# One mixer block in another order: inputs first, gates inside the recurrence, a chunked state space branch

## The chip, the cores and the metric

One core of a Trainium2 chip runs the whole program. The time is device microseconds of one execution, compared by the median of several. Engines run their own queues in order and meet at semaphores: TensorE (PE), VectorE (DVE), ScalarE (ACT), GpSimd (POOL) and SyncE (SP), which issues DMAs.

## The reference

Two transformer blocks at 512 tokens and width 1024. The change lies in the first one's mixer:

```
mod = silu(c) @ ada_w + ada_b            # six groups of 1024: sh1, sc1, gt1, sh2, sc2, gt2
h = rms_norm(x) * (1 + sc1) + sh1
p = h @ w_in                             # inputs of four branches, and four gates of 1024
y_a = rwkv7(...)                         # state S (64x64 a head, 4 heads):
                                         #   S = S*w_t + (S a_t) b_t^T + v_t k_t^T ; o_t = S r_t
y_b = spatial_gating(...)                # gelu, layer norm, a 128x128 causal mix per chunk
y_c = short_conv(...)                    # three taps
y_d = s5(...)                            # 1024 complex states: x_t = a x_{t-1} + B u_t ;
                                         #   y = Re(C x) + d u ; then gelu, a gated projection
merged = sum_i sigmoid(gate_i) * y_i
x = x + gt1 * (merged @ w_o)
```

Then a feed-forward layer with modulation by sh2, sc2 and gt2, and a second block of two layers that the change leaves as it is.

## The kernel before

Activations lie transposed, as 8 tiles of 128 features by 512 tokens. A product is made in three matmuls per 128x128 weight block (high times high, high times low, low times high part; `product`, L1280). Weights come as a stream of pieces of 128x1024, 24 matmuls each: POOL loads the high part, negates it and adds the weights in a second DMA, four slots ahead. The order of the pieces is written out by hand (`mixer_pieces`, L54) and each engine's program follows it. Results go through PSUM banks 0 to 3 in turn; `product` waits until the tile four before has been taken out by its owner. Banks 4 to 7 serve the small matmuls.

Every instruction of DVE and ACT is followed by a wait for itself (`do`), so each of them does one thing at a time. `need` waits for the next count of a semaphore.

The modulation weights `ada` come as 48 slabs of 128x1024, eight for each of the six groups, through four slots; SP loads the next when a slot is free. DVE multiplies each with a column of silu(c) and adds them up (`modulate`, L441), and PE adds the partitions with one-column matmuls (`modulation`, L1310). Groups 0 and 1 come before the first norm, group 2 after the recurrence (after `rw_out`), 3 and 4 beside the output projection, 5 in the feed-forward.

The order in the mixer: conv, gating and state space inputs (12 pieces), the gating branch's layer norm and mix, set-up of the state space branch (transposes, masks and tables of cosines and sines by doubling to length 512 on DVE). Then `for s in range(S5T)`: for each of 8 groups of 128 states PE makes the inputs, DVE rotates, scans over 512 tokens and rotates back, and PE reads out; gates and outputs of the conv and gating branches stand between (`BESIDE`, L65). Then the 7 recurrence inputs, their preparation, padded copies, blocks of small matmuls, a triangular solve of 31 steps on DVE with a transposition through DRAM on either side, and the recurrence over 16 chunks of 32 tokens, all of whose small products are made by PE and copied by DVE (heads 0 and 1) and ACT. Gates and outputs of the state space branch and of the recurrence stand before and after these chains. `gated` (L836) multiplies a branch's tile with its gate and adds it to `merged`.

Of the kernel before, what the change touches and what calls it, by code (L numbers as in the profile page):

```python
# [28 lines left out]
C = 32  # L29
# [8 lines left out]
S5T = 8  # L38

# [79 lines left out]
def build(nc, A, out):  # L119
# [6 lines left out]
    with ExitStack() as ctx:  # L126
# [24 lines left out]
        arena = sb("arena", [P, ARENA])  # L151
        eye_r = sb("eye_r", [P, P], F32R)
# [7 lines left out]
        t_dram = nc.dram_tensor("pair_inverse", (2, H_A, NCK, C // 2, C), F32, kind="Internal").ap()  # L160

# [26 lines left out]

        def gate_room(p):

            at = (ARENA - 4 * T, ARENA - 4 * T, ARENA - 5 * T, 2048 if p < 28 else 4096)[p // 8] + p % 4 * T
            return arena[:, at:at + T]

        merged, product, glu = x, work[:, 0, :], work[:, 1, :]
        ada_m = place([("sum", (2, D)), ("ada", (ADA, D))], at=ARENA - (ADA + 2) * D)
        conv_m = place([("bg", (2, T)), ("cg", (2, T)), ("z", (2, T)), ("y", (2, T))])
        sg_m = place([("z", (4, T)), ("mu", (T,)), ("d", (2, T)), ("sq", (2, T)), ("std", (T,)), ("rstd", (T,)),
                      ("vn", (2, T)), ("vt", (2, 4, P)), ("ws", (4, P)), ("wsm", (4, P)), ("bs", (2, P)),
                      ("mix", (2, T)), ("caus", (P,))], at=4096)
        s5_m = place([("ct", (8, T)), ("st", (8, T)), ("w", (6, T)), ("bt", (2, 8, P)), ("bpad", (2, 8, P)),  # L200
                      ("bb", (2, 8, 16)), ("b_in", (2, 8, 16)), ("m8", (8, 8)), ("c_in", (2, 2, P)), ("u", (2, T))])
        s5_m["cc"] = s5_m["bpad"]
        assert s5_m["end"] <= ARENA - 4 * T
# [9 lines left out]
                       at=max(rw_in["end"], rw_bd["end"]))  # L213
# [34 lines left out]
        def _(sp):  # L248
# [3 lines left out]
            for q in range(ADA):  # L252
                sp.dma_start(ada[:, q, :], A["ada"][q]).then_inc(S(f"ada_in{q}"), 16)
# [733 lines left out]
        def _(act):  # L987
# [114 lines left out]
            for k in range(4):  # L1102
                gate()
# [656 lines left out]
```

## Time and profile before

| | us |
|---|---|
| median of 3 runs (lowest, highest) | 2542.22 (2538.32, 2545.75) |
| the profiled execution | 2537.91 |
| its span | 2536.1 |
| PE busy | 2212.2 (87%) |
| DVE busy | 1420.2 (56%) |
| POOL busy | 845.3 (33%) |
| ACT busy | 441.1 (17%) |
| mean granted TensorE clock | 0.922 |

Busy shares are means over stages with different limits. The first block's mixer takes somewhat over a quarter of the span; the rest is feed-forward, attention and a second block. A granted clock of 1.0 is TensorE's 2.4 GHz, 0.5 is 1.2 GHz.

### The profile page before, as it was taken

The page shows a single profiled execution, that of the slowest core. Times are in us where ns is not written, and L with a number is a line of the kernel's source. Part 1 is how long each engine was busy: PE and PEld are TensorE (multiplying, and loading weights), DVE is VectorE, ACT ScalarE, POOL GpSimd, SP SyncE. Part 2 cuts the span into 40 slices and gives each one's busy share as a digit, 9 for nine tenths or more (in the row PEclk, how much of TensorE's full clock was granted, in tenths as well). Part 3 has the DMA queues.
Part 4 walks back from the last instruction along what each step waited for, and adds up shares of the span by engine and source line. Part 5 has one row for each costly group of instructions (what it writes and reads, how often), then busy time and mean ns, then how long its engine had stood idle before and what let it go on. Part 6 is the DMA issues. An engine that isn't in the chain of part 4 may idle for free.

```text
span 2536.1 us, 26355 instructions
## 1 busy us (share of the span) xinstructions
PE 2212.2 (87%) x10172; PEld 1736.6 (68%) x10172; DVE 1420.2 (56%) x1964; ACT 441.1 (17%) x871; POOL 845.3 (33%) x1009
## 2 busy tenths in 40 slices
PE   1967999668787999999988999999898679999995
PEld 1745667557665888887854787878677338878784
DVE  6459775763567344256545572736563665727364
ACT  1010002101000000021056220201210562202021
POOL 1312333110232444444410444444433004444442
PEclk9978999875797999999987999999999789999998
DMA  7635667530695999998820898989877108989895
GB/s 252 135 65 108 141 136 164 96 80 1 174 298 152 205 193 196 191 193 179 183 61 1 193 193 181 195 177 196 194 163 174 31 1 187 193 179 194 182 194 125
DMA packets 115269, 390.31 MB, mean 154 GB/s; under 512 B 20516, under 2 KB 21412, under 8 KB 114632
## 3 DMA queue, kind: packets, MB, share of 16 engines
q0 software_dynamic: 96624, 350.46, 64.8%
q1 hardware_dynamic: 18520, 38.16, 4.3%
q8 instruction: 81, 1.33, 0.2%
q14 instruction: 44, 0.36, 0.0%
HBM read 385.88 MB, written 2.62 MB: 153 GB/s over the span
## 4 chain that ended last, share of the span: by engine, by line
PE 72%; DVE 17%; DMA 5%; ACT 3%; issue 2%; POOL 0%; SPq 0%; DVEq 0%; ACTq 0%
PE ps L1290 61%; DMA arena<-in_ada 3%; PE ps L1379 2%; PE ps L1360 2%; PE ps L1395 1%; DMA w_lo<-in_w 1%; DVE small L706 1%; DVE arena L450 1%; ACT arena L1231 1%; PE ps L1517 1%; ACT arena L1239 1%; DVE work L555 1%; DVE h_lo L367 1%; DVE arena L733 1%; PE ps L1476 1%
## 5 line engine op out<-in xcount | busy, mean ns | idle before, releaser
L1290 PE MATMUL ps<-h_hi,w_hi 128*128 128x512 f32 x1760 | 713.6, 405 | 39.0 <-DVE h_lo L367 27.9
L1290 PE MATMUL ps<-h_lo,w_hi 128*128 128x512 f32 x1760 | 695.7, 395 | 0.0
L1290 PE MATMUL ps<-h_hi,w_lo 128*128 128x512 f32 x1760 | 694.6, 395 | 0.0
L330 POOL DMA_DIRECT2D w_hi<-in_w x334 | 185.7, 556 | 1516.0 <-PE ps L1290 1515.2
L1290 PEld LDWEIGHTS ps<-h_hi,w_hi 128*128 128x128 f32 x1760 | 336.7, 191 | 132.6 <-DVE h_lo L367 28.3
L1290 PE MATMUL ps<-g_hi,w_hi 128*128 128x512 f32 (+1 forms) x880 | 345.6, 393 | 52.0 <-DVE g_lo L367 21.7
L1290 PEld LDWEIGHTS ps<-h_lo,w_hi 128*128 128x128 f32 x1760 | 337.2, 192 | 74.2 <-issue 6.9
L1290 PEld LDWEIGHTS ps<-h_hi,w_lo 128*128 128x128 f32 x1760 | 336.9, 191 | 71.8
L335 POOL TENSOR_SCALAR w_lo<-w_hi 128x1024 fp32r<-128x1024 f32 x334 | 358.6, 1074 | 35.9 <-DMA w_hi<-in_w 30.1
L1290 PE MATMUL ps<-g_lo,w_hi 128*128 128x512 f32 (+1 forms) x880 | 341.6, 388 | 0.0
L1290 PE MATMUL ps<-g_hi,w_lo 128*128 128x512 f32 (+1 forms) x880 | 341.1, 388 | 0.0
L338 POOL DMA_DIRECT2D w_lo<-in_w x334 | 300.4, 899 | 106.0 <-POOL w_lo L335 106.0
L1290 PEld LDWEIGHTS ps<-g_hi,w_hi 128*128 128x128 f32 x880 | 169.4, 192 | 97.0 <-DVE g_lo L367 24.3
L1290 PEld LDWEIGHTS ps<-g_hi,w_lo 128*128 128x128 f32 x880 | 169.6, 193 | 33.3
L1290 PEld LDWEIGHTS ps<-g_lo,w_hi 128*128 128x128 f32 x880 | 169.5, 193 | 32.6 <-issue 0.7
L1256 ACT ACTIVATE arena<-arena,vec 128x512 f32<-128x512 f32 x88 | 71.8, 816 | 412.2 <-DVE arena L728 404.7
L739 DVE TENSOR_TENSOR x<-ps,x 128x512 f32<-128x512 f32 x48 | 33.2, 692 | 183.9 <-PE ps L1290 183.9
L733 DVE SCALAR_TENSOR_TENSOR arena<-arena,vec 128x511 f32<-128x511 f32 x88 | 113.9, 1294 | 3.6 <-ACT arena L1256 0.6
L728 DVE TENSOR_TENSOR arena<-ps,work 128x512 f32<-128x512 f32 x88 | 60.9, 692 | 91.9 <-PE ps L1290 90.5
L960 DVE TENSOR_TENSOR arena<-arena 128x512 f32<-128x512 f32 x32 | 50.3, 1570 | 77.7 <-ACT arena L1178 77.7
L966 DVE SCALAR_TENSOR_TENSOR x<-ps,mod,x 128x512 f32<-128x512 f32 x32 | 24.0, 751 | 111.6 <-PE ps L1290 111.5
L366 DVE CAST g_hi<-arena 128x512 fp32r<-128x512 f32 (+1 forms) x100 | 80.6, 806 | 6.3 <-ACT arena L1112 2.9
(343 smaller groups left out, 2126.7 us busy)
## 6 DMA issues: line engine op xcount, KB each, us to landing
w_hi<-in_w POOLq DMA_DIRECT2D x334, 512.0 KB, 3.9
w_lo<-in_w POOLq DMA_DIRECT2D x334, 512.0 KB, 5.6
arena<-in_ada SPq DMA_DIRECT2D x48, 512.0 KB, 8.8
x<-in_xT SPq DMA_DIRECT2D x1, 2048.0 KB, 17.3
x<-in_xT SPq DMA_DIRECT2D x4, 512.0 KB, 4.7
arena<-in_memT SPq DMA_DIRECT2D x2, 1024.0 KB, 5.4
out_y<-arena SPq DMA_DIRECT2D x1, 2048.0 KB, 6.3
work<-in_mask_dil SPq DMA_DIRECT2D x1, 640.0 KB, 5.9
```

The source lines that it names most:

```text
L330: pool.dma_start(w_hi[:, q % SLOTS, :], A["w"][q]).then_inc(S(f"high_in{q % SLOTS}"), 16)
L335: pool.tensor_scalar(w_lo[:, q % SLOTS, :], w_hi[:, q % SLOTS, :].bitcast(F32), -1.0, 0.0, ALU.mult, ALU.add).then_inc(S("negated"), 1)
L338: pool.dma_start(w_lo[:, q % SLOTS, :], A["w"][q], accum_op=ALU.add).then_inc(S(f"low_in{q % SLOTS}"), 16)
L366: do(dve.tensor_copy(hi, src))
L728: do(dve.tensor_tensor(cv_m["z"][:, side, :], tile()[:], rstd, ALU.mult), "conv_scaled")
L733: do(dve.scalar_tensor_tensor(dst[:, 1:], z[:, :T - 1], w(1), dst[:, 1:], ALU.mult, ALU.add))
L739: update = lambda k: do(dve.tensor_tensor(x[:, k, :], tile()[:], x[:, k, :], ALU.add), "x_done")
L960: do(dve.tensor_tensor(s, r, r, ALU.mult), "relu_used")
L1256: do(act.activation(c[:, j % 2, :], cv_m["z"][:, side, :], ACT.Identity, scale=V("cw2", at), bias=V("cb2", 44 * layer + 22 * side + j0 + j ...
L1290: mm = pe.matmul(bank, w[:, slot, cols], a(k), start=(k == 0 and i == 0), stop=(k == blocks - 1 and i == 2))
L1360: mm = pe.matmul(bank(g)[:, 0:width], at_m["q"][half(g), pair, P * qb:P * qb + P], keys, start=True, stop=not fox)
L1379: mm = pe.matmul(ps[6 + pair % 2][64 * g:64 * g + 64, q0:T], values, pt[pair % 2][:, g, b, q0:T], start=(b == 0), stop=(b == blocks - 1))
```

## The change

- The pieces come in another order: all 19 input pieces first, then gates and outputs.
- Modulation groups 0, 1 and 2 are made by PE alone: `modulation_piece` multiplies each slab as it lies in its slot with a column of silu(c), 8 matmuls of one column, and sums over 8 slabs in PSUM. Groups 0 and 1 are split 12 and 4 slabs, with state space set-up between. Group 2's transfers start after the last chunk, and PE takes its slabs after the last branch output.
- `norm` has its rounding to the high part, with the shift, done by ACT (`high_shifted`); DVE makes the low part. Both norms of the first block use it.
- The state space branch works in chunks of 8 tokens: within a chunk by a Toeplitz matrix (made by matmuls from powers of the step, and spread through DRAM), between chunks by one rotate, scan, rotate back over 64 chunks for all 8 groups of states at once, 512 columns. Its input and its output are turned through DRAM, by one transfer out and 16 in each time. The tables are 64 long.
- In the recurrence PE issues after each of a chunk's three stages a step of six 512-column matmuls of gates and outputs; DVE and ACT have a step of the gating between their copies, with some turns skipped. The chain's first products move from banks 0 and 1 to 4 and 5.
- Single gate pieces stand between the blocks of small matmuls; nine pieces stand before the recurrence instead of four. Clearing the padded tiles moves from DVE (8192 elements, and 2048 later) to ACT.
- Buffers in the arena are laid out anew, with one more tile of 512.

```diff
 def mixer_pieces():
-    order = [("conv_in", 6), ("sg_in", 4), ("s5_in", 2)]
-    for branch in ("conv", "sg"):
-        order += [(branch + "_gate", 4), (branch + "_out", 1)] * 2
-    order += [("rwkv_in", 7)] + [("s5_gate", 4), ("s5_out", 2)] * 2
-    return order + [("rwkv_gate", 4), ("rwkv_gate", 4), ("rwkv_out", 1), ("rwkv_out", 1)]
-BESIDE = [(2, None), (2, 0), (2, None), (2, 1), (1, None), (1, None), (1, None), (1, 1)]
+    order = [("conv_in", 6), ("sg_in", 4), ("s5_in", 2), ("rwkv_in", 7)]
+    order += [("conv_gate", 4), ("conv_out", 1)] * 2
+    order += [("sg_gate", 4), ("sg_out", 1), ("sg_gate", 4), ("s5_gate", 4), ("sg_out", 1)]
+    order += [("s5_gate", 1), ("s5_out", 1)] * 4
+    return order + [("rwkv_gate", 8), ("rwkv_out", 2)]
...
+                sp.dma_start(ada_first[:, q, :], A["ada"][q]).then_inc(S(f"ada_in{q}"), 16)
             sp.dma_start(x[:], A["xT"]).then_inc(S("x_in"), 16)
             for q in range(ADA, 16):
-                sp.wait_ge(S("ada_used"), q - ADA + 1)
-                sp.dma_start(ada[:, q % ADA, :], A["ada"][q]).then_inc(S(f"ada_in{q % ADA}"), 16)
-            sp.wait_ge(S("ada_used"), 16)
+                sp.wait_ge(S("ada_taken"), q - ADA + 1)
+                sp.dma_start(ada_first[:, q % ADA, :], A["ada"][q]).then_inc(S(f"ada_in{q % ADA}"), 16)
...
+            sp.dma_start(u_dram.rearrange("g p k j n -> (g p) (k j n)"), s5_m["u"].rearrange("p k j n -> p (k j n)")).then_inc(S("scratch_out"), 16)
+            sp.wait_ge(S("scratch_out"), 48)
+            for r in range(Q):
+                for k in range(2):
+                    sp.dma_start(s5_m["u_turned"][16 * r:16 * r + 16, 8 * k:8 * k + 8, :],
+                                 u_dram[:, :, k, Q - 1 - r, :].rearrange("g p n -> p g n")).then_inc(S("s5_u_in"), 16)
...
-            sp.wait_ge(S("rw_out"), 2)
+            sp.wait_ge(S("rec_o"), NCK)
             for q in range(16, 48):
-                if q >= 16 + ADA:
-                    sp.wait_ge(S("ada_used"), q - ADA + 1)
+                if 16 + ADA <= q < 24 + ADA:
+                    sp.wait_ge(S("ada_taken"), q - ADA + 1)
+                elif q >= 24 + ADA:
+                    sp.wait_ge(S("ada_used"), q - ADA - 24 + 1)
...
+                def low(k):
+                    need("h_high")
+                    do(dve.scalar_tensor_tensor(h_lo[:, k, :], work[:, 4 + k % 2, :], shift(k), h_hi[:, k, :].bitcast(F32),
+                                                ALU.add, ALU.subtract), "h_ready")
                 for k in range(KT):
-                    t = work[:, 4 + k % 2, :]
-                    do(dve.scalar_tensor_tensor(t, x[:, k, :], gain(k), work[:, 3, :], ALU.mult, ALU.mult))
-                    if shift is not None:
-                        do(dve.tensor_scalar(t, t, shift(k), None, ALU.add))
-                    both_parts(h_hi[:, k, :], h_lo[:, k, :], t, "h_ready")
+                    do(dve.scalar_tensor_tensor(work[:, 4 + k % 2, :], x[:, k, :], gain(k), work[:, 3, :], ALU.mult, ALU.mult), "norm_scaled")
+                    if k:
+                        low(k - 1)
+                low(KT - 1)
...
+                def step_beside():
+                    u = turn[0]
+                    turn[0] += 1
+                    if u not in (0, 10, 16, 18, 24, 26, 32, 34):
+                        next(steps, None)
...
-                decay = mag[:, s:s + 1].broadcast_to((P, T))
-                do(dve.tensor_tensor_scan(w[:, 2, :], decay, w[:, 0, :], 0.0, ALU.mult, ALU.add))
-                do(dve.tensor_tensor_scan(w[:, 3, :], decay, w[:, 1, :], 0.0, ALU.mult, ALU.add))
...
+                do(dve.tensor_tensor_scan(w[:, 2 + part, :], decay, w[:, part, :], 0.0, ALU.mult, ALU.add))
...
+            def modulation_piece(q, slots):
+                pe.wait_ge(S(f"ada_in{q % ADA}"), 16 * (q // ADA + 1))
+                for k in range(8):
+                    col = q // 8 * 8 + k
+                    mm = pe.matmul(PA[:, col:col + 1], slots[:, q % ADA, P * k:P * k + P], small[:, 0, q % 8:q % 8 + 1],
+                                   start=(q % 8 == 0 and k == 0), stop=(q % 8 == 7 and k == 7), skip_group_check=True)
+                mm.then_inc(S("ada_taken"), 1)
...
+            for q in range(12):
+                modulation_piece(q, ada_first)
...
+            for i in range(4):
+                for s in range(4):
+                    mm = pe.transpose(ps[i][:, P * s:P * s + P], m["f"][:, i // 2, 4 * (i % 2) + s, :], K("ident"))
+                mm.then_inc(S("s5_turned"), 1)
...
+            for q in range(12, 16):
+                modulation_piece(q, ada_first)
             total_squares(work[:, 2, :])
-            modulation(0)
-            modulation(1)
...
+            pe.wait_ge(S("s5_u_in"), 32 * Q)
+            pe.wait_ge(S("sg_y"), 2)
...
+            pe.wait_ge(S("s5_toep"), 1)
+            need("s5_states")
+            for s in range(S5T):
+                for g in range(2):
+                    cols = slice(NQ * s, NQ * s + NQ)
+                    pe.matmul(ps[6 + g][:, cols], m["toep"][:, 2 * s + g].rearrange("p j c -> p (j c)"), m["u_turned"][:, 2 * s + g, :],
+                              start=True, stop=False)
+                    for part in range(2):
+                        mm = pe.matmul(ps[6 + g][:, NQ * s + 1:NQ * s + NQ], m["g"][halves[g], part, s, :],
+                                       m["w"][halves[g], part, NQ * s:NQ * s + NQ - 1], start=False, stop=(part == 1))
+            mm.then_inc(S("s5_outputs"), 2)
+            project(2, "dve_freed")
...
             blocks(pad("a"), pad("b"), 64, 8)
+            project(1, "gate")
             blocks(pad("k"), pad("a"), 64, 8)
...
+            branch_out(1, 4)
             project(4, "gate")
+            project(4, "gate")
+            def beside():
+                y = lambda b: (lambda k: g_hi[:, 2 * b + k, :], lambda k: g_lo[:, 2 * b + k, :])
+                slot = open_piece()
+                for i in range(4):
+                    yield from product_steps(slot, 2, *y(1), "gated", first_block=2 * i, first=(i == 0))
+                for _ in range(4):
+                    yield from product_steps(open_piece(), 8, *h, "gate")
+                    slot = open_piece()
+                    for i in range(4):
+                        yield from product_steps(slot, 2, *y(2), "glu_gate" if i % 2 else "gated", first_block=2 * i, first=(i == 0))
+                for _ in range(4):
+                    yield from product_steps(open_piece(), 8, *h, "gate")
+            steps = beside()
...
+                next(steps, None)
...
                 mm.then_inc(S("rec_o"), 1)
-            project(3, "gate")
+                next(steps, None)
+            for _ in steps:
+                pass
+            project(4, "gate")
...
             pe.wait_ge(S("rw_out"), 2)
-            for half in range(2):
-                branch_out(3, 4)
-            modulation(2)
+            branch_out(3, 8)
+            for q in range(16, 24):
+                modulation_piece(q, ada_m["ada"])
             project(7, "x_done", ready=lambda k: need("merged"))
```

## Rows read from the trace of the kernel before

**Rows 1.** the page's 40 slices: PE busy and granted clock, in tenths

```profile
PE   1967999668787999999988999999898679999995
...
PEclk9978999875797999999987999999999789999998
```

**Rows 2.** stages: from:to, length, PE PEld DVE ACT POOL, clock, DMA, GB/s

```profile
140.40:356.30 215.90, 168.33 (x614) 119.80 (x613) 181.21 (x280) 17.59 (x27) 51.67 (x60) 0.84 0.47 99
...
557.10:633.10 76.00, 67.99 (x513) 54.02 (x513) 23.65 (x94) 13.50 (x62) 0.00 (x0) 0.50 0.00 1
633.10:709.00 75.90, 58.03 (x247) 46.81 (x246) 48.40 (x62) 5.61 (x9) 18.25 (x21) 0.79 0.66 172
709.00:795.00 86.00, 62.45 (x229) 45.87 (x230) 55.07 (x71) 7.03 (x10) 19.97 (x24) 0.76 0.73 227
795.00:2536.00 1741.00, 1617.18 (x7233) 1277.70 (x7232) 914.61 (x1163) 350.62 (x696) 659.77 (x785) 0.96 0.76 163
```

**Rows 3.** ACT in order of time (start, us), one gate in each piece

```profile
458.73 0.60 ACT L1091 ACTIVATE arena<-ps 128x512 f32<-128x512 f32 x1 [4.85 <-PE ps L1290]
```

**Rows 4.** PE's waits up to 720 us: total, times, longest

```profile
PE ps L1322 <- DVE work L374: 40.1, 1, 40.1
...
PE ps L1517 <- DVE arena L521: 18.5, 1, 18.5
...
PE ps L1550 <- DVE work L564: 8.0, 16, 0.5
```

**Rows 5.** all engines in order of time, the first 82 us

```profile
40.09 2.05 PE L1322 MATMUL ps<-work,con 128*128 128x512 f32 x2 [40.09 <-DVE work L374]
...
44.73 3.35 DVE L406 RECIPROCAL work<-work 128x512 f32<-128x512 f32 x1
...
53.55 3.58 PE L1314 MATMUL ps<-con,arena 128*128 128x1 f32 x16 [8.21 <-DVE small L452]
...
60.14 0.75 DVE L412 SCALAR_TENSOR_TENSOR work<-x,small,work 128x512 f32<-128x512 f32 x1
...
62.64 0.75 DVE L412 SCALAR_TENSOR_TENSOR work<-x,small,work 128x512 f32<-128x512 f32 x1
...
78.25 0.63 PE L1290 MATMUL ps<-h_lo,w_hi 128*128 128x512 f32 x1
...
79.41 0.69 DVE L800 COPY arena<-ps 128x512 f32<-128x512 f32 x1 [1.81 <-PE ps L1290]
```

**Rows 6.** PE's groups by form, 136 to 182 us: count, busy us, mean ns

```profile
L1421 PE MATMUL ps<-con,arena 128*128 128x128 f32 x8 | 2.2, 434 | 7.1 <-DVE arena L825 7.1
```

**Rows 7.** one stretch inside L1568, columns as in rows 2

```profile
652.00:664.00 12.00, 12.00 (x70) 11.55 (x70) 4.26 (x7) 0.60 (x1) 0.89 (x2) 0.64 0.18 36
```

**Rows 8.** PE in order of time, blocks and start of the recurrence

```profile
489.77 9.98 PE L1517 MATMUL ps<-arena 128*64 128x64 f32 x256 [18.52 <-DVE arena L521]
...
508.80 6.99 PE L1517 MATMUL ps<-con,arena 128*64 128x64 f32 x128 [5.55 <-DVE arena L546]
...
557.11 0.48 PE L1541 MATMUL ps<-arena 64*64 64x64 f32 x4 [19.34 <-DMA arena<-pair_inverse]
```

**Rows 9.** DMA issues from 494 to 512 us: KB each, median us to landing

```profile
arena<-pair_scores SPq DMA_DIRECT2D x8, 64.0 KB, 4.0
```

**Rows 10.** DVE in order of time, first and last of the solve's 62 operations

```profile
516.81 1.39 DVE L555 TENSOR_TENSOR work<-arena 128x32 f32<-128x32 f32 x1
...
548.82 0.69 DVE L556 TENSOR_REDUCE arena<-work 128x16 f32<-128x512 f32 x1
```

**Rows 11.** the chain that ended last, 640 to 700 us: start, us

```profile
652.06 10.02 PE ps L1568 x64
...
667.16 12.62 DMA arena<-in_ada
...
687.25 0.70 DVE work L841
...
689.88 0.70 DVE work L841
```

More of the change, by code:

```diff
@@ L1100, in glu_gate, with clear @@
                 count[1] += 1
-            for k in range(4):
-                gate()
-            skip(4)
-            for gates, branch in BESIDE:
-                for k in range(gates):
-                    gate()
-                if branch is not None:
-                    skip(4)
-            for k in range(2):
-                need("s5_sum")
-                do(act.activation(m["w"][:, 2 + k, :], m["w"][:, k, :], ACT.Gelu_apprx_tanh), "s5_gelu")
+            def clear(i):
+                do(act.activation(rw_pad["all"][:, 2048 * i:2048 * i + 2048], K("ident")[:, 0:1].broadcast_to((P, 2048)), ACT.Copy, scale=0.0),
+                   "rw_cleared")
             v = rw_in
@@ L1147, in _ @@
                 do(act.activation(v["e"][:, 0], v["cum"][:, k], ACT.Exp, scale=-1.0), "rw_exp")
-            act.wait_ge(S("bd_used"), 18)
+            skip(4)
             for f in range(4):
+                gate()
+            skip(4)
+            for f in range(8):
                 gate()
@@ new lines, in adapted @@
+            def adapted(rows, first_bank, after=None):
+                for k in range(2):
+                    if after is not None:
+                        pe.wait_ge(S(after), k + 1)
+                    pe.matmul(ps[first_bank + k][:], lora[rows, P * k:P * k + P], v["m"][rows, :],
+                              start=True, stop=True).then_inc(S("rw_adapted"), 1)
+            adapted(slice(0, 32), 4)
+            adapted(slice(32, 64), 6)
+            project(2, "gate")
+            adapted(slice(64, 128), 4, "rw_decay")
@@ L1464, in _ @@
             pe.wait_ge(S("conv_y"), 2)
             branch_out(0, 4)
-            for s, (gates, branch) in enumerate(BESIDE):
-                project(gates, "gate")
-                if s < S5T - 1:
-                    need("s5_bu_used")
-                    inputs(s + 1)
-                if branch is not None:
-                    pe.wait_ge(S("sg_y" if branch else "conv_y"), 2)
-                    branch_out(branch, 4)
-                need("s5_states")
-                for part in range(2):
-                    mm = pe.matmul(ps[6 + s // 4][:], m["cc"][:, part, s, :], m["w"][:, 4 + part, :],
-                                   start=(s % 4 == 0 and part == 0), stop=(s % 4 == 3 and part == 1))
-                mm.then_inc(S("s5_read"), 1)
@@ L1561, in _ @@
                 mm.then_inc(S("rec_o"), 1)
-            project(3, "gate")
+                next(steps, None)
+            for _ in steps:
+                pass
+            project(4, "gate")
             pe.wait_ge(S("o_padded"), 2)
```

590 lines of the change are left out of this document (356 added, 234 removed).

## The prediction

> **What bounds the kernel now.** The page's slices came first [rows 1]: TensorE (PE) is near full in most of the 40 slices, but among the first eleven stand ones, sixes and sevens, and the granted clock dips with them. Then the span cut into stages [rows 2]: after 795 us PE is busy 1617 of 1741 us, and the change touches nothing there. Before 795 it is busy 595 of 795. So the question is the mixer, and in it not PE's work but its waits and its slow clock: 0.84 granted in the state space stage (140.4 to 356.3), 0.50 in the recurrence, 0.79 up to the merged sum.
>
> A piece of 24 matmuls takes 5.44 us at full clock (0.60 of work and 4.85 of waiting between two gates) [rows 3]; the mixer's 61 pieces are 332 us. They take from 79.3 (first tile done) to 709 (last merge), 630 us. The other 300 are VectorE (DVE) chains, latencies and small matmuls; the longest waits of PE are listed in [rows 4]. The sums below are of one execution, span 2536.1, 2537.9 with what lies around it, 0.2% below the median of 2542.2. A difference under 0.3% could not be told from none.
>
> **Prologue: loses 21 us.** Before, PE has nothing until 40.1 us, DVE sums the first modulation, and the norm begins after 8 matmuls of one column, at 57.7 [rows 5]. Now each of 16 slabs is 8 such matmuls on PE: 3.58 us a slab [rows 5], 57 us in all. In order: 12 slabs from about 9 us, when the first can have landed (estimate), to 52; 16 transposes at 0.28 [rows 6] to 56.5; 32 small products, 64 records of 0.12 (the recurrence puts 32 records in a chunk of 4.75 less some 1 us of waits) [rows 2, 4], to 64; 4 slabs to 78.5. ScalarE (ACT) copies those transposes ahead of its squares, so the squares run 64 to 71, under the 4 slabs. Then the sum of squares 2, root and latencies 2.6, reciprocal 3.35 [rows 5], modulation 0.4: the norm starts near 86.5. DVE's extra set-up, some 17 us of small operations, lies beside the 12 slabs and is free; without that cover DVE would be ready at 31 us. The norm gets shorter: a tile took 2.50 us on DVE [rows 5]; with the rounding on ACT, DVE has two operations of 0.75 and gaps, 1.56. 8 tiles 12.5, a last triple of slow matmuls 1.3: first tile done at 100 instead of 79.3.
>
> Bounds of a slab: 3.58 at the low clock, 1.79 at the high one, after which data decide. I take 3.58, since this form is only seen at that pace, and since dense small matmuls let the clock fall: in L1568 PE was busy throughout 652 to 664 and was granted 0.64 [rows 7]. The Trainium skill ("TensorE: Matmul & The Clock Gate", Part 1: The HAM clock gate) has the array throttled by default and lets activity release it. Read plainly, 57 us of busy PE would then run at 2.4 GHz. This trace leans the other way, and the plain reading is the first rival.
>
> **Inputs together: to 227.** 18 more pieces, 98 us. PE's small work beside them: mean and variance 3, 8 transposes 2.2, mixing 4, state space inputs (64 records, 0.039 each as the 256 of L1517 [rows 8], or 0.12: 2.5 to 7.7, I take 5), its outputs (96 records, 0.04 to 0.22, the latter a one-column matmul's per record: 4 to 21, I take 11 for the full weights): 25. One wait for the layer norm and the clock's recovery: 4. What goes is the state space stage, in which DVE was busy 181 of 216 us and PE 168 [rows 2]: tables to length 512, sixteen masked copies, eight rounds of rotate, scan, rotate back. In their place one round at 512 columns, 11 us, under two pieces. The tables to 64, 21 us, go under four pieces. Two trips through DRAM of 16 transfers each: at 0.5 to 0.7 us to issue, each is 14 to 17 us, and PE has about 24 and 20 us of other work meanwhile. Lower bound no cost. Upper: all 16 landing one after the other at 4.0 us [rows 9], 45 us exposed each. I take none, since such transfers were issued without waiting for each other.
>
> **Gates to the padding: to 305.** 10 pieces 54.4, lora and head sums 6.5: 288. Then the padding, for which PE waited 18.5 [rows 4]; DVE has the same chain after its gates, so 17 again. The clearing of the padded tiles moves from DVE to ACT, in four parts beside gates: 0, or up to 7 if they delay the exponentials. Lora's transfer comes earlier and is late nowhere.
>
> **Blocks and inverse: to 397.** Blocks 18 us for both bursts [rows 8], four pieces between them 21.8, wait for the padded v 3: 348. Nine pieces, 49 us, to 397. On DVE meanwhile: four gates till 355, the solve 32.9 to 388 [rows 10], the trip to DRAM and back 7.6 (548.8 + 0.7 to 557.1) [rows 8] to 396. The old wait of 19.3 is covered, with 1 us to spare; what is late next is this same trip, at 1 us for each us that the gates take longer.
>
> **Recurrence: to 492.** Before, 76 us for 16 chunks at clock 0.50 [rows 2], with pieces elsewhere. Now three steps of six 512-column matmuls stand in each chunk: 4.08. The chunk's records at the high clock: half of 3.7, 1.85. Its waits of 0.5 [rows 4] lie under steps of 1.36. 5.95 a chunk, 95 us. Each step adds, on DVE and ACT, an operation of 0.69 or 0.60 ahead of the chain's next copy, and PE waits behind it for that copy; DVE has 3.8 us of work in the 5.95. Bounds: 5.95, and 11.9 with everything at the low clock; I take the lower end, because these matmuls are those of the stretches with a clock of 1.0.
>
> **To the merged sum: 556.** 4 steps and 4 gates 27.2 (covering the layer norm on DVE) to 519; L1568 10.0 and the last bonus 3.7 [rows 11]: 533. First branch tile 2.6, 8 merges of 2.63 [rows 11]: 556. The third modulation stood between, on DVE, from 667.2 to 687.3, waiting for its slabs; its transfers now start after the last chunk. That 20 us goes, but PE takes the slabs after the branch tiles, which wait for banks until 546: 8 x 3.58 = 28.6, to 575. The first tile of the output projection is at 581.5, 25 after the merge instead of 4.
>
> **After it.** The other modulations stay on DVE at the pace of the DMAs; four slabs and x are in place earlier, -4. The second norm is 7.5 shorter. So the 86 us from the last merge to 795 [rows 2] become 86 + 21.5 - 4 - 7.5 = 96.
>
> Sum: +21, then 630 becomes 456, -174, then +10: **-143, 2395 us**.
>
> **Rivals.**
> - *One-column matmuls raise the clock.* Slab 1.79: 12 slabs and set-up by 40, squares to 48, norm at 59.5, first tile 73 (-27 against my sum), and 14 less before the projection: 2354. For: PE without a gap for 57 us. Against: rows 7. Chance 0.18.
> - *The clock stays low in the recurrence.* 11.9 a chunk, +95: 2490. For: 0.50 over 76 us. Against: it begins behind nine dense pieces and has few gaps. 0.06.
> - *Something small is late:* both DRAM trips exposed by 17, or chunks of 8 us: +35, 2430. 0.13.
> - *Slower.* Steps and chain serialize: each engine's queue holds a wait for the step's tile ahead of the chain's copy. A chunk is then 4.75 and three rounds of PE 2.56 (low clock), ACT 0.60, DVE 0.69, 11.6: 16.3, +166 in all, 2561, which is 23 slower. It decides from 14.9 a chunk (143/16 more). For: DVE and ACT do take turns in a fixed order. Against: they skip turns so as to lag behind PE. 0.03.
> - *Merge and slabs eat the gain:* within 0.3%. 0.02.
>
> **Numbers.** My forecast has 0.58. With the first and third rival **2345 to 2450** holds eight in ten; outside are the low-clock recurrence and the tails. Faster 0.95, same 0.02, slower 0.03.
>
> **What shows it.** One-column matmul records 0.22 apart (0.11: first rival) and the first tile near 100; granted clock 1.0 through the recurrence and DVE's state updates 5.95 apart; PE's wait for the padding about 17, for the inverse under 3; 28 us of slabs before the output projection. I am wrong if the prologue costs nothing or a chunk exceeds 8 us.

## The result and the profile after

The changed kernel takes 2462.35 us (median of 4, 2457.46 to 2475.3) beside 2542.33 for the one before on the same chip: a ratio of 0.9694, 95% interval 0.9653 to 0.9735. That is 80 us faster, where 143 had been forecast. 2462 lies above the range of 2345 to 2450. The profiled execution took 2457.46, its span is 2455.7.

The stages of the changed kernel, cut at the marks of the forecast (columns as in [rows 2]: from:to, length, PE, PEld, DVE, ACT, POOL, clock, DMA share, GB/s):

```profile
98.10:207.00 108.90, 98.56 (x496) 78.58 (x495) 70.48 (x149) 9.97 (x12) 40.35 (x48) 0.98 0.79 166
207.00:232.00 25.00, 24.99 (x97) 21.50 (x97) 2.90 (x4) 0.00 (x0) 0.00 (x0) 0.55 0.00 0
232.00:324.00 92.00, 75.41 (x308) 58.19 (x308) 52.98 (x66) 34.20 (x39) 30.40 (x36) 0.91 0.71 149
324.00:425.20 101.20, 92.67 (x760) 78.07 (x760) 54.84 (x98) 8.48 (x13) 32.72 (x39) 0.96 0.75 151
425.20:552.90 127.70, 127.67 (x795) 90.52 (x795) 45.90 (x126) 22.04 (x76) 30.18 (x36) 0.98 0.49 100
552.90:640.10 87.20, 83.69 (x393) 73.76 (x393) 37.75 (x53) 6.82 (x11) 22.09 (x24) 0.78 0.72 191
640.10:714.00 73.90, 57.64 (x228) 42.80 (x227) 52.90 (x54) 12.91 (x19) 22.13 (x24) 0.84 0.78 230
714.00:2455.00 1741.00, 1612.64 (x7232) 1276.44 (x7230) 914.97 (x1163) 351.89 (x696) 661.36 (x785) 0.96 0.76 163
```

The last line answers to the last of [rows 2]: 1741 us there too, so all of the gain is ahead of it. The fifth line is the recurrence with its steps. PE is busy in all of it at a clock of 0.98, VectorE in a third, ScalarE in a sixth: whatever makes it 127.7 us instead of the forecast 95 is in PE's own queue. The second line is one block of small products at a clock of 0.55.

PE's four longest waits up to 700 us, which answer to [rows 4] (total, times, longest):

```profile
PE ps L1713 <- DVE arena L575: 16.6, 1, 16.6
PE ps L1500 <- DMA arena<-in_ada: 13.9, 2, 10.4
PE ps L1459 <- DVE h_lo L455: 11.0, 5, 8.5
PE ps L1758 <- DMA arena<-pair_inverse: 5.8, 1, 5.8
```

The 40.1 of the first norm is gone, the 19.3 of the inverse is 5.8 (under 3 had been forecast), and the 18.5 of the padding stays as 16.6, as forecast.

One chunk of the recurrence on PE, in order of time (start, us; dense matmuls are L1459, six to a step; each small fp32 product leaves two records, so x2 is one product and x4 is two):

```profile
473.64 0.50 PE L1459 MATMUL ps<-g_hi,w_hi 128*128 128x512 f32 x1
473.98 0.39 PE L1459 MATMUL ps<-g_lo,w_hi 128*128 128x512 f32 x1
...
474.90 0.40 PE L1459 MATMUL ps<-g_hi,w_lo 128*128 128x512 f32 x1
475.23 0.33 PE L1758 MATMUL ps<-arena 64*64 64x64 f32 x2
475.49 0.33 PE L1759 MATMUL ps<-work,arena 128*64 128x64 f32 x2
475.75 0.32 PE L1758 MATMUL ps<-arena 64*64 64x64 f32 x2
476.00 0.33 PE L1759 MATMUL ps<-work,arena 128*64 128x64 f32 x2
476.26 0.50 PE L1459 MATMUL ps<-g_hi,w_hi 128*128 128x512 f32 x1
...
477.85 0.33 PE L1765 MATMUL ps<-work,arena 64*64 64x64 f32 x4
478.11 0.50 PE L1459 MATMUL ps<-g_hi,w_hi 128*128 128x512 f32 x1
...
479.70 0.45 PE L1769 MATMUL ps<-arena 64*128 64x64 f32 x4
479.98 0.40 PE L1771 MATMUL ps<-work,arena 64*128 64x64 f32 x4
480.30 0.33 PE L1773 MATMUL ps<-work,arena 128*64 128x64 f32 x2
...
481.56 0.50 PE L1459 MATMUL ps<-h_hi,w_hi 128*128 128x512 f32 x1
```

From 473.64 to 481.56 is 7.92 us. A step takes 1.59 (473.64 to 475.23), not 1.36: its first matmul is followed after 0.34 instead of 0.227, and the next small product comes 0.33 behind its last one. Three steps are 4.77. The remaining 3.15 us are sixteen small products: 1.03, 0.26, 0.60 and 1.26. The four products of L1758 and L1759 follow each other in pairs of records and take 1.03 us, while the two of L1765 together take 0.26. A half is two of the four heads; it has its own 64 rows, its own 64 columns of a result, or both.

### The profile page after: what moved, and what is told of

It reads as the page before. It is cut to its first block, busy times and chain, and to the rows that moved or that the text cites. A ratio compares the mean times of both kernels' runs of the same rounds, so it can differ in the third digit from the quotient of the medians.

```text
span 2455.7 us, 27262 instructions
## 1 busy us (share of the span) xinstructions
PE 2246.5 (91%) x10664; PEld 1787.2 (73%) x10664; DVE 1284.3 (52%) x1822; ACT 467.0 (19%) x897; POOL 849.3 (35%) x1009
## 4 chain that ended last, share of the span: by engine, by line
PE 77%; DVE 12%; DMA 5%; ACT 3%; issue 2%; POOL 0%; SPq 0%; DVEq 0%; ACTq 0%
PE ps L1459 63%; PE ps L1500 3%; DMA w_lo<-in_w 2%; PE ps L1565 2%; PE ps L1546 2%; PE ps L1581 1%; DMA w_hi<-in_w 1%; DVE small L786 1%; DMA arena<-in_ada 1%; PE ps L1713 1%; DVE work L611 1%; ACT arena L1407 1%; ACT arena L1399 1%; DVE arena L813 1%; PE ps L1657 1%
## 5 line engine op out<-in xcount | busy, mean ns | idle before, releaser
L1459 PE MATMUL ps<-h_hi,w_hi 128*128 128x512 f32 x1760 | 706.2, 401 | 26.8 <-DVE h_lo L455 20.4
L1459 PE MATMUL ps<-h_lo,w_hi 128*128 128x512 f32 x1760 | 689.5, 392 | 0.0
L1459 PE MATMUL ps<-h_hi,w_lo 128*128 128x512 f32 x1760 | 689.3, 392 | 0.0
L1459 PEld LDWEIGHTS ps<-h_hi,w_hi 128*128 128x128 f32 x1760 | 332.9, 189 | 116.1 <-issue 26.2
L1459 PE MATMUL ps<-g_hi,w_hi 128*128 128x512 f32 (+1 forms) x880 | 347.6, 395 | 42.3 <-DVE g_lo L409 24.8
L1459 PEld LDWEIGHTS ps<-h_hi,w_lo 128*128 128x128 f32 x1760 | 332.9, 189 | 71.0
L1459 PEld LDWEIGHTS ps<-h_lo,w_hi 128*128 128x128 f32 x1760 | 333.4, 189 | 69.9 <-issue 4.1
L1459 PE MATMUL ps<-g_lo,w_hi 128*128 128x512 f32 (+1 forms) x880 | 341.8, 388 | 0.0
L1459 PE MATMUL ps<-g_hi,w_lo 128*128 128x512 f32 (+1 forms) x880 | 341.4, 388 | 0.0
L1459 PEld LDWEIGHTS ps<-g_hi,w_hi 128*128 128x128 f32 x880 | 169.4, 193 | 85.1 <-DVE g_lo L409 27.5
L1459 PEld LDWEIGHTS ps<-g_hi,w_lo 128*128 128x128 f32 x880 | 169.4, 192 | 33.8
L1459 PEld LDWEIGHTS ps<-g_lo,w_hi 128*128 128x128 f32 x880 | 169.5, 193 | 31.9 <-issue 0.2
L1500 PE MATMUL ps<-small,arena 128*128 128x1 f32 x384 | 79.3, 344 | 13.9 <-DMA arena<-in_ada 13.9
L1500 PEld LDWEIGHTS ps<-small,arena 128*128 128x128 f32 x384 | 79.2, 321 | 14.1 <-issue 10.4
```

Of the source, the lines that this page charges most:

```text
L1459: mm = pe.matmul(bank, w[:, slot, cols], a(k), start=(k == 0 and i == 0), stop=(k == blocks - 1 and i == 2))
L1500: mm = pe.matmul(PA[:, col:col + 1], slots[:, q % ADA, P * k:P * k + P], small[:, 0, q % 8:q % 8 + 1], start=(q % 8 == 0 and k == 0), stop ...
```

## Experiments

The table gives marks on VectorE's rows of each profiled execution, in us: start of the first norm's reciprocal, last operation of the padding, first copy behind the chain's second product in the recurrence (the rows of L642), length of a chunk (15 of them, averaged between these copies), first tile of the output projection, first hidden tile, and the rest to the end of the span. The last column is the median time; its pair of before was 2541.8 (rows 2 to 5), 2543.3 (rows 6 to 9) and 2542.8 (the last four).

```
kernel     norm  padded  chain  chunk  w_o    hidden  rest    median
changed    80.4  323.3   430.3  7.95   640.1  714.6   1741.1  2462.4
rec_plain  80.4  323.7   428.0  5.70   663.5  738.6   1742.3  2488.3
rec_two    83.4  328.0   435.6  7.43   641.2  715.8   1742.8  2462.9
rec_lean   81.1  325.7   433.5  7.71   639.7  713.2   1744.6  2459.8
outputs    84.6  320.7   427.0  7.94   636.6  711.2   1740.8  2450.2
rec_order  83.3  328.0   434.8  7.47   637.5  712.0   1745.6  2452.2
rec_alt    80.5  324.1   429.1  6.85   621.6  696.2   1745.1  2446.8
late       83.3  327.9   435.3  7.94   640.9  717.4   1759.4  2458.9
dve8       76.0  320.5   427.5  7.94   637.0  710.3   1745.6  2458.4
late2      81.0  323.9   431.3  7.94   626.0  702.8   1753.5  2454.6
dve8b      56.7  306.6   414.1  7.94   622.6  698.2   1751.1  2444.2
alltwo     83.4  326.6   434.0  6.78   629.8  705.2   1743.6  2451.6
combo      57.4  295.4   402.3  6.77   580.4  656.2   1750.9  2404.2
```

The rest, which no kernel touches, differs by up to 19 us from one execution to the next, and the first norm by 3 to 4 us among kernels with the same instructions up to it. So the length of an edited stage says more of an edit than the whole does. Each length comes from one profiled execution.

### What the interleaving earned

All steps out of the recurrence, four ahead of it and the others behind:

```
-                next(steps, None)      (three times in each chunk, on PE)
+            for _ in range(4):
+                next(steps)            (ahead of the recurrence)
```

> The changed kernel with all steps taken out of the recurrence: the first four (branch products of 6 matmuls) stand ahead of it, the other 48 behind it. This asks what the interleaving earned and what the chain's own products cost without it. Theory (PE's issue of the small products and the switch between them and the 512-column matmuls bound the recurrence, and a small product costs nearly the same at either clock): a chunk takes 4.7 us as before the change at a granted clock near 0.5, of which about 3.3 is PE's own work and 1.4 waits for copies; the recurrence is 75 us instead of 127.7 and the steps, 48 x 1.36 less the four moved, take some 62 behind it, so the whole is about 9 us slower than the changed kernel: 2471. Rival (the products follow the clock and would take 6.3 us a chunk at 0.5): a chunk of 7 us or more, 112 us, whole 2507. My recorded reasoning (3.7 of work at the low clock, 1.85 at the high one) gives the same chunk as the theory here, but then the loss inside the steps has to be the steps' own.

Measured: 2488.28 (ratio to before 0.9793, 0.976 to 0.9826), 26 us slower than the changed kernel. The chunk is 5.70 at the low clock:

```profile
425.60:517.00 91.40, 83.69 (x513) 66.22 (x514) 24.27 (x97) 13.52 (x63) 0.00 (x0) 0.51 0.01 2
```

Theory and rival both missed the chunk: it is neither the 4.7 of before nor 7. The interleaving works, but the chain itself has grown by 0.95 us a chunk, against [rows 2] (76 us for 16). The first products of one chunk on PE, here and then in the kernel before, show where:

```profile
448.42 0.47 PE L1763 MATMUL ps<-work,arena 128*64 128x64 f32 x2
448.82 0.47 PE L1762 MATMUL ps<-arena 64*64 64x64 f32 x2
449.23 0.47 PE L1763 MATMUL ps<-work,arena 128*64 128x64 f32 x2
450.17 0.48 PE L1768 MATMUL ps<-work,arena 64*64 64x64 f32 x4 [0.47 <-DVE work L641]
```

```profile
599.82 0.42 PE L1541 MATMUL ps<-arena 64*64 64x64 f32 x2
600.16 0.48 PE L1545 MATMUL ps<-work,arena 128*64 128x64 f32 x4
```

The change had swapped two loops: the two products of one half now stand next to each other, where before the constant products of both halves came first and then those of the state. Pairs of records 0.41 apart stand where four records of both halves (L1545) stood in one row. The loops of the state update were swapped as well: from L1768 to the first output product it is 1.91 us instead of 1.49. That is 0.42 of the growth, and the other 0.5 or so is in the first products. The forecast had not read this edit in the diff.

### The third place of a step, and the price of a product

```
+                next(steps, None)      (second step, third right behind it)
...
-                next(steps, None)      (behind the output products)
```

> The changed kernel with the third step of each chunk issued directly behind the second, so that a chunk has two places with dense matmuls instead of three; the output products of a chunk then run straight into the next chunk's first products. Theory (each place costs 0.36 us in which PE waits for nothing that the profile shows, and about 0.1 us more for a slow first matmul): 16 x 0.47 = 7.5 us less, chunk 7.45, 2455. Rival 1 (the gap is only the tail of the dense matmuls, modelled late, and not lost time): no change, 2462. Rival 2 (the third place covered the state update's copy on DVE, 0.5 us a chunk): the gap gained is lost again, 2462 or up to 5 us slower, and the waits of PE on DVE's state update show it.

Measured: the chunk 7.42 between two like rows of PE in the middle of the recurrence (as for every chunk below; the changed kernel's is 7.92), 0.50 less, as the theory has it; but 2462.94 in all, no change. By the marks the recurrence is 7.8 us shorter, it began 5.3 us later (3.0 of it at the first norm, which the edit does not touch), and the path from the last chunk to the output projection is 3.6 us longer (94.1 instead of 90.5). There PE shows 1.9 us of waits for weights, which the changed kernel does not have.

```
-                    pe.matmul(..., bd["rkT"][rows[p], c, :], bd["vt"][rows[p], c, :], start=False, stop=True)
```

> The changed kernel with two of the sixteen small products of each chunk left out (the part of the output that comes from the values inside the chunk; the output is not the reference's). It prices a small product at the high clock with everything else in place. Theory (PE is bound by its own issue, 3.15 us for 32 records, 0.1 us each): 4 records x 16 chunks x 0.1 = 6.3 us less, chunk 7.53, 2456. Rival (a chain of copies, or the switches alone, sets the chunk, and the products stand beside it): no change, 2462. If the clock had halved the products as I forecast, 0.06 each, 3.7 us less.

The stop flag moves to the product before. Measured: 7.69 a chunk, 0.23 less for 4 records, 0.058 each; 2459.77 in all, which cannot be told from the changed kernel. Those 0.058 are the figure the forecast had used (half of 0.12), not the theory's 0.1. So a product at the margin costs what was forecast, and the average of 0.1 has something else in it.

### The order of the products

```
+                need("state_set", 2 if c else 1)
                 for p in range(2):
-                    need("state_set", 1 if c or p == 0 else 0)
                     pe.matmul(ps[4 + p]..., bd["akT"]..., bd["vt"]..., start=True, stop=False)
+                for p in range(2):
                     pe.matmul(ps[4 + p]..., pad("a")(p, c), state[:, now, p, :], start=False, stop=True)
```

> The changed kernel with the order of the small products in a chunk as it was before the change: first the chunk's constant product of both 64-row halves and then the state's product of both, and so for the state update; the change had put the two products of one half next to each other. Theory (two products of different halves run beside each other, 0.26 us for both, two of the same half take 0.26 each; the chunk without steps took 5.70 us after the change and 4.75 before it, at the same low clock): the first four products take 0.52 instead of 1.03 us, the chunk 7.4 instead of 7.92, 8 us less, 2454. Rival (the 0.95 us are the price of waiting for both state updates ahead of the first product, since the product now writes into the bank that they read): no change, 2462.

> The same, and the six output products of a chunk alternate between the halves too (before and after the change each half's three stood together). Theory: their 1.26 us become about 0.75, the chunk 6.9, 16 us less than the changed kernel, 2446. Rival (only products that wait for nothing between them gain): as the kernel with the first order alone.

In both kernels the two products of the state update are split into two loops in the same way. In rec_alt the three output products of each half are split into three such loops as well.

Measured: rec_order 7.41 a chunk and 2452.22 (ratio 0.9644). All of its 0.51 us is in the first four products; the state update takes 0.59 instead of 0.60, so its split gains nothing here. In rec_alt, where the outputs alternate too, a chunk is 6.80 and the whole 2446.84 (0.9616, 0.9597 to 0.9635). A chunk of rec_alt, dense rows left out:

```profile
474.88 0.33 PE L1758 MATMUL ps<-arena 64*64 64x64 f32 x4
475.14 0.34 PE L1760 MATMUL ps<-work,arena 128*64 128x64 f32 x4
477.00 0.33 PE L1766 MATMUL ps<-work,arena 64*64 64x64 f32 x4
478.85 0.44 PE L1770 MATMUL ps<-arena 64*128 64x64 f32 x4
479.12 0.39 PE L1773 MATMUL ps<-work,arena 64*128 64x64 f32 x4
479.44 0.34 PE L1775 MATMUL ps<-work,arena 128*64 128x64 f32 x4
479.71 0.33 PE L1777 MATMUL ps<-work,arena 64*64 64x64 f32 x4
479.87 0.28 PE L1779 MATMUL ps<-arena 64*64 64x64 f32 x4
481.68 0.33 PE L1758 MATMUL ps<-arena 64*64 64x64 f32 x4
```

Now four records stand in every row and the first four products take 0.52 instead of 1.03. Two products of different halves run beside each other; two of one half follow each other. The wait for both state updates, the rival, costs nothing that can be seen while the third step stands in its place: it is in rec_order as well.

The Trainium skill ("TensorE: Matmul & The Clock Gate", Part 3: Packing small matmuls — row/col tiling) says that a weight load overlaps with matmuls in flight only where the row group differs. The products of 64 rows (L1758 at 474.88, L1766) agree with it. Those of L1760 and L1775 do not fit it as it stands: both halves use all 128 rows and differ only in the 64 columns of the result, and still four records take 0.26 and 0.27 us, where two took 0.26 with both products of a half in a row. The measurement decides: here different columns were enough.

With the third step moved as well:

> The changed kernel with all small products of a chunk alternating between the halves and the third step directly behind the second: both edits to the recurrence at once. If the two add up as measured (7.92 to 7.42 for the step; 7.92 to 6.80 for the order), a chunk takes 6.3 us and the whole is 26 us below the changed kernel: 2437. If instead the alternation only used time that the third place would have cost anyway, 6.8: 2446.

Measured: 6.74 a chunk, 2451.55. The two edits do not add up: once the products alternate, the third place costs 0.06 us. The rows of PE tell why. In rec_two half of the 0.50 came because the outputs of one half could run beside the first products of the next chunk (the small products on both sides of the border take 2.64 us instead of 1.86 and 1.03), the other half because two steps in a row take 2.94 us instead of twice 1.59. With alternating products the first gain is no longer there to be had. The second is, but 0.17 of it goes again: the first product of a chunk starts at 479.17, behind VectorE's state update (478.51, two operations, 0.60), 0.38 after the last output row, where 0.21 is the usual distance. So the rival of rec_order, the wait for both updates, does cost something once no step covers it.

### The block of output products

```
-            for s in range(S5T):                 (96 records in a row, then two pieces)
+            steps = two_pieces()
+            for s in range(S5T):
                 ...
+                next(steps)
```

> The changed kernel with the state space branch's output products (96 records, 24.6 us in one block) cut into eight parts, one ahead of each of the eight steps of the two input pieces that follow. Theory (the block lets the clock fall; its first records took 0.36 and 0.58 a group of 2 and 4, its later ones 0.62 and 1.04): at the high clock 16 x 0.94 = 15 us, and 8 switches of 0.47, 3.8: 19 in place of 24.6, 6 us less, 2456. Rival (such products cost the same at either clock and the pace changed for another reason): 24.6 + 3.8, 4 us more, 2466.

Measured: 2450.21 (0.9638, 0.9609 to 0.9667). From the last operation on the states to the padding it is 110.0 us instead of 117.1 (320.7 less 210.7; 323.3 less 206.2), 7 less, near the 6 of the theory. The whole is 12 less, more than this stage explains. The granted clock in the changed kernel, and then in this one (5 us each):

```profile
205.00:210.00 5.00, 2.99 (x18) 2.68 (x18) 4.79 (x7) 0.00 (x0) 0.00 (x0) 0.93 0.30 60
210.00:215.00 5.00, 5.00 (x20) 4.30 (x19) 0.01 (x1) 0.00 (x0) 0.00 (x0) 0.50 0.00 0
```

```profile
215.00:220.00 5.00, 5.00 (x17) 4.05 (x16) 0.00 (x0) 0.00 (x0) 2.51 (x3) 0.50 0.68 129
220.00:225.00 5.00, 5.00 (x21) 4.14 (x21) 0.00 (x0) 0.00 (x0) 0.00 (x0) 0.74 0.41 80
225.00:230.00 5.00, 5.00 (x29) 4.16 (x28) 0.44 (x1) 0.00 (x0) 0.00 (x0) 1.00 0.00 0
```

In both it falls at the first products. Between dense steps it is back at its high level by 225 us and stays there; in one block it is at 0.50 until the block ends at 231.9. PE had waited 2.3 us just ahead of the first product in both, so these rows alone do not tell whether the wait or the products let the clock fall; the small products of the next section, with no wait ahead of them, do.

### The slabs behind the last branch

```
-            branch_out(3, 8)
-            for q in range(16, 24):
-                modulation_piece(q, ada_m["ada"])
...
+                    product(slot, 2, *y3, "gated", first_block=2 * i, first=(i == 0))
+                    modulation_piece(16 + 4 * q + i, ada_m["ada"])
```

> The changed kernel with the eight slabs of the third modulation group one by one between the eight output tiles of the last branch, instead of in a row behind them, where they took 24 us at a clock that fell to 0.50. Theory (dense matmuls between them keep the clock up, and VectorE's merges, 2.63 us a tile against 1.4 of PE, leave PE idle there): a slab costs 1.7 to 2.0 us, eight tiles and slabs 29 us in place of 11 and 24; the first tile of the output projection 8 to 12 us earlier, 2452. Rival (a one-column product costs the same between dense matmuls, 3.0 to 3.4 us a slab): nothing to gain, 2462. Rival 2 (the second four slabs wait for their transfers, which start when a slot is free): half of it, 2457.

Measured: 2458.94, which cannot be told from the changed kernel, and a profile that has both clocks in it (slab and first matmul of the next tile, at the low clock and then at the high one):

```profile
601.81 3.41 PE L1500 MATMUL ps<-small,arena 128*128 128x1 f32 x16
605.08 0.77 PE L1459 MATMUL ps<-g_hi,w_hi 128*128 128x512 f32 x1
...
623.06 1.84 PE L1500 MATMUL ps<-small,arena 128*128 128x1 f32 x16
624.76 0.48 PE L1459 MATMUL ps<-g_hi,w_hi 128*128 128x512 f32 x1
```

A slab is 3.27 us at the low clock and 1.70 at the high one, whose price no row of before had. The clock had fallen in the 32 small products ahead (L1786). The changed kernel shows the same fall with no wait in it: PE is busy throughout, at a granted clock of 0.98 from 580 to 585 us and of 0.50 from 585 to 590, with L1786 from 581.9. In the profile of late, tiles and slabs then went on in turns at the low clock from 599.1 to 619.7 before it rose. With the small products spread over the steps of the last two gates:

```
-            project(4, "gate")
+            project(2, "gate")
+            steps = two_gates()        (a step behind every fourth small product)
```

> As the kernel with the slabs between the last branch's tiles, and also the 32 small products ahead of that branch (64x32, 8.5 us in a row) stand in eight groups between the steps of the last two gate pieces. In that kernel's profile the clock fell in those small products, the first four tiles and slabs ran at the low clock (2.57 and 3.27 us) and the other four at the high one (1.38 and 1.71 to 1.84). Theory (a run of small products lets the clock fall, dense matmuls between them keep it): 8 x (1.4 + 1.8) = 26 us for branch and slabs and 6 for the small products, 12 to 15 us less than the changed kernel, 2449. Rival (the clock falls by chance, at either place): no steady gain, 2459 as before, with times that scatter over 20 us.

Measured: all eight slabs take 1.84 us each by their rows and stand 3.17 us apart with their dense work (from 595.33 to 617.50), and the output projection comes 75.6 us behind the last chunk's copy instead of 90.5: 15 less, as the theory has it. The rival, a clock that falls by chance, would have scattered over 20 us; the four runs lie within 8 (the six of late within 22). The whole is 2454.60, 8 less than the changed kernel; the profiled execution's rest was 12 us longer than the changed kernel's.

### The prologue

```
-            for q in range(12):
-                modulation_piece(q, ada_first)
+            for q in range(8):
+                first_piece(q)         (the other eight: one operation each on VectorE)
```

> The changed kernel with the second modulation group's eight slabs summed on VectorE (1.28 us each, as before the change) among its set-up operations, and the first group's eight on TensorE; they are loaded in turns. Theory (16 slabs at 3.43 us on PE, 55 us, are what delays the first norm, and PE's clock is at its low level through them although the profile prints 1.0): PE has 28 us of slabs, 3.6 and 7.0 of transposes and small products, all done near 53; sum of squares, root and reciprocal bring the norm to 60 instead of 84: 24 us less, 2438. Rival (VectorE becomes the bound, with 17 us of set-up, 10 of slabs, 7 of tables, 6 of squares): norm near 62 to 68, 16 to 22 less. Rival 2 (the transfers bound it, 13 MB at some 370 GB/s): 45 us and no later than the theory.

Measured: 2458.43, the norm at 76.0: only 4 us. With half of the slabs gone, the norm waited for something else. ScalarE's rows:

```profile
57.57 2.48 ACT L1213 ACTIVATE arena<-ps 128x512 f32<-128x512 f32 x4 [46.76 <-PE ps L1630]
64.50 0.59 ACT L1216 ACTIVATE arena<-ps 128x128 f32<-128x128 f32 x2 [4.45 <-PE ps L1635]
65.12 1.95 ACT L1155 ACTIVATE work<-x 128x512 f32<-128x512 f32 x3
```

It had been idle for 46.76 us, with the squares (L1155) queued behind two sets of copies that came from PE.

```
+            rms_x()
             need("s5_turned", 4)
             ...
-            rms_x()
```

> As the kernel with the second group's slabs on VectorE, with the squares taken as soon as x has landed (they had stood behind ScalarE's copies of the state space tables, from 65 us), x loaded behind the eighth slab, and the transposes and small products of the state space set-up behind the sum of squares; VectorE builds the second table after the norm. Theory (the order on ScalarE, not the slabs, was late in that kernel: PE had finished slabs at 53.8 and products at 64.4, but the squares ended at 71): the last slab is used near 48 to 52, root and reciprocal end at 60 instead of 79 and of 84 to 88, the first tile comes at 75 instead of 98; 22 us less than the changed kernel, 2440. Rival (the transfers, 13 MB, end later than that): slabs until 56, 15 us less, 2447.

Measured: 2444.24 (0.9601, 0.9578 to 0.9623). The norm is at 56.7, 24 us earlier; at the padding 16.7 are left. VectorE's second table, moved behind the norm, holds the first tiles' copies back and the clock is 0.91 from 80 to 100. The slabs themselves are paced by their transfers: PE waits 24.4 us for them, 10.7 of it for the first.

### All of it

> All edits together: second group's slabs on VectorE with early squares, output products of the state space branch between the steps of two pieces, both edits to the recurrence, slabs and small products of the last branch between dense matmuls. If each term stands by itself (22 + 8 + 26 + 13) the time is 69 us below the changed kernel, 2393, which is where my forecast for the change lay; if the inverse's trip becomes the next wait, since PE reaches it earlier and VectorE doesn't, 8 us of it are lost: 2401.

Measured: 2404.17, ratio to before 0.9451 (0.9429 to 0.9473), 58 us below the changed kernel. That is slower than both sums, 2393 and 2401. The inverse's wait is 6.6 us and the one for the padding 16.6, hardly more than in the changed kernel, so the wait that was expected to grow didn't. By the marks, the 11 us that are missing from the first sum are 8 in the recurrence (101.5 us between its first and last copy instead of 119.3: 18 less, as in alltwo, where 26 had been expected) and 4 in the prologue (the last operation on the states is 18 us earlier, not 22). The block of output products brings 10 instead of 8, the last branch 14 instead of 13, and 1 is lost behind it. PE's waits for weights are 9.0 us, 3.2 in the changed kernel.

## Why the forecast was wrong

The direction, the untouched remainder and most steps held; the size did not. Against the forecast's marks, each difference being the stage's own:

- **Prologue**: first tile at 98.1, forecast 100. That it came so near is in part luck: PE waited 3.5 us for the fifth slab, which the sum does not have, and the 32 small products took 4.0 us instead of 7.7 (7.0 in rec_two). The rival that one-column matmuls raise the clock is out. Eight slabs without a gap took 3.43 us each (PE in order of time):

```profile
27.68 27.47 PE L1500 MATMUL ps<-small,arena 128*128 128x1 f32 x128 [3.47 <-DMA arena<-in_ada]
```

  The granted clock of the same stretch:

```profile
30.00:40.00 10.00, 10.00 (x48) 10.00 (x48) 3.71 (x4) 0.00 (x0) 0.00 (x0) 1.00 0.81 263
```

  It is printed as 1.00, yet the pace is the one of the low clock, 3.27 to 3.43 a slab against 1.70. The last four slabs have the same pace (13.81 us, 3.45 each), and there the column has come down to the low clock:

```profile
70.00:80.00 10.00, 8.23 (x32) 6.65 (x32) 7.33 (x6) 1.68 (x2) 0.00 (x0) 0.50 0.42 44
```

  So the column can't be believed ahead of the first change of the clock; the duration of a known form can. By the plain reading of the Trainium skill ("TensorE: Matmul & The Clock Gate", Part 1: The HAM clock gate) the activity of these slabs would have released the clock; eight slabs in a row at the low pace speak against it.
- **Inputs**: 245 instead of 227. Of it 14 is the block of output products, 24.9 instead of 11, and 2 more the pieces behind it, which began at the low clock (13.3 instead of 10.9). The forecast took a value between two ends for full weights; at the pace of its first records (207.01 to 208.88 for two of sixteen groups) it would have been 15, and then the clock fell. That falling clock was seen in [rows 7] and used for the slabs, but not here.
- **Gates to the padding**: 1 more; the wait was 16.6, forecast 17.
- **Blocks and inverse**: 9 more. 3 in the blocks; the inverse left VectorE at 413.4 and PE went on at 425.2, 11.8 us instead of the 7.6 of the forecast, which is most of the 5.8 of wait. One us to spare was too little to be called cover.
- **Recurrence**: the step that failed, 127.7 instead of 95, half of the whole error. A chunk was 7.95 us, so even the prediction's own sign, one above 8, did not show it. The clock (0.98) and the lack of waits were right, and so was the price of a product at the margin. Wrong was "The chunk's records at the high clock: half of 3.7, 1.85": they took 3.15. A smaller part is the step, 1.59 instead of 1.36, as PE turns from one kind to the other and back: 0.69 for three (two steps in a row take 2.94, not 3.18). Of the 1.30 in the small products, 0.51 is the change putting products of one half next to each other, shown by restoring the order. 0.27 is the misread row: the waits in a chunk of before were 0.5 [rows 4], not 1 as the forecast took, so half of the work was 2.12. 0.25 is the third step, which stands between the outputs and the next chunk's first products; in rec_two they overlap again. The last, nearly 0.3, no run isolates.
- **To the output projection**: 87.2 us instead of 89.5. A slab was 3.0, forecast 3.58.
- **Behind it**: 74 instead of 70.5; the remainder as forecast.

Stage by stage -2, 20, 1, 9, 33, -2 and 3 make 62 us; the profiled execution lies 5 us below the median, which makes the 67.

The third rival had chunks of 8 us in it and a price of 35 with the DRAM trips; the chunks came, the trips were free (PE never waited for them). The rival of steps and chain in turns (16.3 a chunk) is out: a chunk is 7.95, and in the changed kernel's recurrence VectorE and ScalarE wait for PE, never PE for them.

## What to carry to other kernels

Where small matmuls use half of the rows or of the columns, let neighbours in the queue be of different halves: the same sixteen products took 3.15 us in one order and 2.01 in the other. Read a diff for the order of loops, not only for what is added and moved. Work put between the steps of a latency chain is not free even where the chain never waits; price a step by its first matmul and the gap behind it. Spread a long run of small products between dense ones: as one block of 25 us, or of 10, it ran at half the clock and handed the low clock on; and before an engine's work is made lighter, look whether the late work stands behind another wait in some queue.

## What was not expected of the hardware

- The granted clock reads 1.00 from 10 to 50 us of the span (changed kernel, rec_two, outputs, dve8, dve8b), at the pace of the low one.
- The same 64 records of products of 16 columns behind the slabs took 3.97 us in one execution and 7.01 in another of the same instructions up to there, and the first norm moved by 3 us with them:

```profile
58.60 3.97 PE L1601 MATMUL ps<-arena 64*128 64x16 f32 x64
62.50 13.81 PE L1500 MATMUL ps<-small,arena 128*128 128x1 f32 x64
```

```profile
58.57 7.01 PE L1601 MATMUL ps<-arena 64*128 64x16 f32 x64
```

  The first pair is the changed kernel, the last row rec_two. The four slabs behind have the low pace in both (13.81 us).
- A one-column fp32 matmul of 128x128 weights takes 0.41 to 0.43 us at the low clock and 0.21 to 0.23 at the high one (3.27 and 3.41, 1.70 and 1.84 for 8). Through the slabs at 30 to 40 us the weight loads are busy as long as PE (10.00 of 10 us), so the weights look like what it costs; no run isolates it.
